# Mamba sample states: streamed past column tiles, updated two sequences at a time

## The reference, cut to what matters

```python
def step(h, inp):
    x_q, dt_q, b_q, c_q = inp
    acum = jnp.cumsum(dt_q * a_gr, axis=1)
    ...
    y = jnp.einsum('bijgr,bjgrp->bigrp', cb[..., None] * lmat, xdt)
    y = y + jnp.einsum('bign,bgrpn->bigrp', c_q, h) * jnp.exp(acum)[..., None]
    to_end = jnp.exp(acum[:, -1:] - acum)
    h = h * jnp.exp(acum[:, -1])[..., None, None] \
        + jnp.einsum('bjgn,bjgrp->bgrpn', b_q, xdt * to_end[..., None])
    return h, y
```

## Time and profile before

| what | value |
|---|---|
| median of the runs | 3171.85 us (3167.19 to 3178.89) |
| the profiled execution's own time (its span, first to last instruction) | 3169.1 us |
| busy share of PE, DVE, ACT, POOL over the span | 85%, 51%, 34%, 6% |
| stretch of the sample part, first read to last add | 1942.9 to 2057.7 us |

### The profile page before, as it was taken

One profiled execution on the slowest core, in us unless ns is written; L12 is line 12 of the kernel. 1 busy time (PEld: TensorE's weight loads), 2 busy tenths in 40 slices (PEclk: granted clock), 3 DMA queues, 4 the chain that ended last, 5 costly groups with the idle time before them and its releaser, 6 DMA issues. The chain is left out here.

```text
span 3169.1 us, 48791 instructions
## 1 busy us (share of the span) xinstructions
PE 2695.0 (85%) x21151; PEld 2385.4 (75%) x21151; DVE 1607.7 (51%) x2358; ACT 1070.8 (34%) x1798; POOL 174.8 (6%) x176
## 2 busy tenths in 40 slices
PE   6939985998847899979989888978997939985999
PEld 5728854998724678869989866678997718864999
DVE  5384336644362577756434843265536374326643
ACT  4333112433311344434334620044434332203442
POOL 0020011000000000000000132200000020011000
PEclk8969867999865899989999965589998978967999
DMA  4210001444200222214434301323442210001442
GB/s 152 90 66 3 6 28 60 153 147 159 98 0 0 67 67 67 67 54 157 149 124 146 138 27 63 131 99 120 147 147 104 83 40 30 6 27 53 147 151 105
DMA packets 44133, 275.70 MB, mean 87 GB/s; under 512 B 5216, under 2 KB 5248, under 8 KB 14096
## 3 DMA queue, kind: packets, MB, share of 16 engines
q1 hardware_dynamic: 43680, 271.95, 24.1%
q0 software_dynamic: 240, 0.64, 0.1%
HBM read 256.32 MB, written 16.24 MB: 86 GB/s over the span
## 5 line engine op out<-in xcount | busy, mean ns | idle before, releaser
L315 PE MATMUL banks<-rounded,rounded 128*128 128x320 f32 x3184 | 1009.8, 317 | 165.3 <-DVE rounded L331 69.1
L316 PE MATMUL banks<-rounded,rounded 128*128 128x320 f32 x3184 | 995.7, 313 | 0.0
L317 PE MATMUL banks<-rounded,rounded 128*128 128x320 f32 x3184 | 995.2, 313 | 0.0
L305 DVE TENSOR_TENSOR rounded<-weight_ring,rounded 128x1024 fp32r<-128x1024 f32 x398 | 487.2, 1228 | 513.4 <-ACT rounded L298 513.1
L315 PEld LDWEIGHTS banks<-rounded,rounded 128*128 128x128 f32 x3184 | 609.4, 191 | 177.3 <-DVE rounded L331 74.3
L316 PEld LDWEIGHTS banks<-rounded,rounded 128*128 128x128 f32 x3184 | 609.7, 191 | 3.6
L317 PEld LDWEIGHTS banks<-rounded,rounded 128*128 128x128 f32 x3184 | 608.8, 191 | 0.0
L298 ACT ACTIVATE rounded<-weight_ring 128x1024 fp32r<-128x1024 f32 x398 | 419.2, 1058 | 414.6 <-PE banks L317 360.1
L942 PE MATMUL banks<-arena 64*64 64x64 f32 x4032 | 146.3, 225 | 22.8 <-PEq L788 20.3
L942 PEld LDWEIGHTS banks<-arena 64*64 64x64 f32 x4032 | 134.4, 140 | 31.0 <-issue 29.2
L470 ACT ACTIVATE arena<-banks 128x320 f32<-128x320 f32 x128 | 56.0, 438 | 247.9 <-PE banks L317 247.9
(11 more groups left out here) (361 smaller groups left out, 3593.1 us busy)
## 6 DMA issues: line engine op xcount, KB each, us to landing
weight_ring<-in_panels SPq DMA_DIRECT2D x206, 1024.0 KB, 4.7
arena<-in_pages SPq DMA_DIRECT2D x64, 320.0 KB, 3.4
arena<-in_ssm SPq DMA_DIRECT2D x8, 1024.0 KB, 4.8
out_ssm_sample<-arena SPq DMA_DIRECT2D x8, 1024.0 KB, 3.8
arena<-in_wkv SPq DMA_DIRECT2D x2, 2048.0 KB, 8.2
out_wkv_sample<-arena SPq DMA_DIRECT2D x2, 2048.0 KB, 6.2
consts<-in_consts SPq DMA_DIRECT2D x1, 1673.5 KB, 9.7
residual<-in_x SPq DMA_DIRECT2D x1, 1280.0 KB, 5.6
```

The source lines that it names most:

```text
L305: self.k.nc.vector.tensor_tensor(self.k.w_lo[:, i % SPLIT], self.raw(i), self.k.w_hi[:, i % SPLIT].bitcast(F32), ALU.subtract)\
L315: mm(out, hi, x_hi, start=start, stop=False)
L316: mm(out, hi, x_lo, start=False, stop=False)
L317: return mm(out, lo, x_hi, start=False, stop=stop)
```

## The change

There are four state buffers: the two old ones, and two more over the first 4096 columns of `XBC`, the convolved inputs, which are last read by the sample chunk's outputs. The sequences go in the order 0, 4, 1, 5, 2, 6, 3, 7, in four pairs.

The read is turned round. The state is the moving operand, 512 columns of a group at a time, and `C` is the weights: for each sequence a 128x32 block per group (`CM`) that holds the eight columns of `C` at the sequence's place among four and zeros elsewhere. The four groups write to four different 32-row strips of one bank, so they sit in four column tiles of the array. The reads of four sequences add up in one bank.

The sums are 32 tokens deep in place of 64: sequence 0 to 3 lie in token rows 0 to 31, sequence 4 to 7 in rows 32 to 63, and a pair takes one of each, in two row tiles, into two banks. Three pairs of banks rotate, and DVE adds 512 columns at a time.

POOL clears and fills `CM` over the prompt state's space after that state's store has landed. Since the reads now come out token by row, ACT copies them to SBUF, PE transposes them, and DVE multiplies them in by four small instructions for each half.

```diff
+    add("seq4", (p[:, None] % 32 // 8 == np.arange(4)[None]))
...
+    HB += [k.at(MB["XBC"] + 2048 * i, MH, 64) for i in range(2)]
+    CM = HT.rearrange("p a b -> p (a b)")[:, 0:1024].rearrange("p (b g t) -> p b g t", b=NB, g=4)
+    YTK = XDT.rearrange("p a b -> p (a b)")[:, 0:1024].rearrange("p (h n) -> p h n", h=2)
+    seqs = [0, 4, 1, 5, 2, 6, 3, 7]
+    sums = [0, 1, 2, 3, 6, 7]
...
-            for b in range(NB):
-                sp.wait_ge(*vec_did.at("HB", b))
-                sp.dma_start(io["ssm_sample"][b], flat(HB[b % 2])).then_inc(state_out[b % 2], 16)
-                if b + 2 < NB:
-                    sp.wait_ge(state_out[b % 2], 16 * (b // 2 + 1))
-                    sp.dma_start(flat(HB[b % 2]), io["ssm"][b + 2]).then_inc(state_in[b % 2], 16)
-            sp.wait_ge(prompt_out, 16)
+            sp.wait_ge(*vec_did.at("y", 2, 7))
+            for s in range(2, 4):
+                sp.dma_start(flat(HB[s]), io["ssm"][seqs[s]]).then_inc(state_in[s], 16)
+            for s in range(NB):
+                sp.wait_ge(*vec_did.at("HB", s, 3))
+                sp.dma_start(io["ssm_sample"][seqs[s]], flat(HB[s % 4])).then_inc(state_out[s % 4], 16)
+                if 1 <= s <= 4:
+                    sp.wait_ge(state_out[s - 1], 16)
+                    sp.dma_start(flat(HB[s - 1]), io["ssm"][seqs[s + 3]]).then_inc(state_in[s - 1], 16)
...
-            for b in range(NB):
-                cols = slice(TP + TS * b, TP + TS * b + TS)
-                pe.wait_ge(state_in[b % 2], 16 * (b // 2 + 1))
-                for f in range(MT):
-                    ins = mm(k.ps[:, 4 + f // 8, (f % 8) * 64 + TS * b:(f % 8) * 64 + TS * b + TS], flat(HB[b % 2])[:, f * P:(f + 1) * P],
-                             XBC[:, 20 + f // 4, cols], start=True, stop=True)
-                ins.then_inc(*pe_did.tick("ys", b))
-                pe.wait_ge(*vec_did.at("bm", b))
-                if b:
-                    pe.wait_ge(*vec_did.at("HB", b - 1))
+            pe.wait_ge(*pool_did.at("cm"))
+
+            def reads(s):
+                b = seqs[s]
+                pe.wait_ge(state_in[s % 4], 16 * (s // 4 + 1))
                 for g in range(4):
-                    ins = mm(k.bank(g), BM[b % 2][0:64, g, :], flat(XDW)[0:64, 512 * g:512 * (g + 1)], start=True, stop=True)
-                ins.then_inc(*pe_did.tick("hb", b))
+                    ins = mm(k.ps[32 * g:32 * g + 32, 4 + b // 4, :], CM[:, b, g, :], flat(HB[s % 4])[:, 512 * g:512 * (g + 1)],
+                             start=b % 4 == 0, stop=b % 4 == 3)
+                ins.then_inc(*pe_did.tick("ys", s))
+
+            def sums_of(pair, g):
+                u = 4 * pair + g
+                if u >= 3:
+                    pe.wait_ge(*vec_did.at("HB", 2 * ((u - 3) // 4) + 1, (u - 3) % 4))
+                for i in range(2):
+                    r = slice(32 * i, 32 * i + 32)
+                    ins = mm(k.bank(sums[u % 3 * 2 + i]), BM[pair % 2][r, g, :], flat(XDW)[r, 512 * g:512 * (g + 1)],
+                             start=True, stop=True)
+                ins.then_inc(*pe_did.tick("hb", pair, g))
...
+            for half in range(2):
+                act.wait_ge(*pe_did.at("ys", 6 + half))
+                s.activation(YTK[:, half, :], k.bank(4 + half), ACT.Copy).then_inc(*act_did.tick("ytk", half))
...
+            pool.wait_ge(prompt_out, 16)
+            g_.memset(flat(HT)[:, 0:1024], 0.0).then_inc(*pool_did.tick("cm0"))
+            pool.wait_ge(*pool_did.at("cm0"))
+            for i in range(4):
+                ins = g_.tensor_copy(CM[:, i::4, :, TS * i:TS * i + TS].rearrange("p b g t -> p g b t"),
+                                     XBC[:, 20:24, TP:T].rearrange("p g (b t) -> p g b t", b=NB)[:, :, i::4, :])
+            ins.then_inc(*pool_did.tick("cm"))
...
+                for g in range(4):
+                    u = 4 * pair + g
+                    vec.wait_ge(*pe_did.at("hb", pair, g))
+                    for i in range(2):
+                        s = 2 * pair + i
+                        if g == 0:
+                            vec.wait_ge(*pool_did.at("hb", s))
+                        part = flat(HB[s % 4])[:, 512 * g:512 * (g + 1)]
+                        v.tensor_tensor(part, part, k.bank(sums[u % 3 * 2 + i]), ALU.add).then_inc(*vec_did.tick("HB", s, g))
```

More of the change, by code:

```diff
@@ L2174, in stage_mamba_scan @@
     act_did, pe_did, vec_did, pool_did = k.tallies("act", "pe", "vec", "pool")
-    state_in = [k.sem("ssm_in_a"), k.sem("ssm_in_b")]
-    state_out = [k.sem("ssm_out_a"), k.sem("ssm_out_b")]
+    state_in = [k.sem(f"ssm_in{i}") for i in range(4)]
+    state_out = [k.sem(f"ssm_out{i}") for i in range(4)]
     prompt_out = k.sem("ssm_prompt_out")
@@ new lines, in _ @@
+            for pair in range(NB // 2):
+                reads(2 * pair)
+                reads(2 * pair + 1)
+                pe.wait_ge(*vec_did.at("bm", pair))
+                for g in range(4):
+                    sums_of(pair, g)
+            for half in range(2):
+                pe.wait_ge(*act_did.at("ytk", half))
+                pe.wait_ge(*vec_did.at("HB", NB - 1, 1))
+                for a in range(4):
+                    ins = nc.tensor.transpose(k.ps[:, 2 + half, a * P:(a + 1) * P], YTK[:, half, a * P:(a + 1) * P], k.const("ident"))
+                ins.then_inc(*pe_did.tick("ysT", half))
@@ L2309, in _ @@
                     g_.tensor_tensor(m, m, bcm(CB[0:n, q // 2, 0:n], 4), ALU.mult).then_inc(*pool_did.tick("m", c, q))
[L2310 to L2312 removed]
+            pool.wait_ge(prompt_out, 16)
[5 more added lines that the diff above has]
+            ins.then_inc(*pool_did.tick("cm"))
+            for s in range(NB):
+                pool.wait_ge(*pe_did.at("ys", s))
+                g_.tensor_tensor(HB[s % 4], HB[s % 4], bc(EE[:, 2 + seqs[s], :], 64), ALU.mult).then_inc(*pool_did.tick("hb", s))
         @block.vector
@@ L2370, in _ @@
             vec.wait_ge(*act_did.at("bt", 2))
[L2371 to L2381, removed]
+            for pair in range(NB // 2):
+                if pair >= 2:
+                    vec.wait_ge(*pe_did.at("hb", pair - 2, 3))
+                v.tensor_scalar(flat(BM[pair % 2])[0:64, :], flat(BT)[0:64, :], k.const("seq4", slice(0, 64))[:, pair:pair + 1],
+                                None, ALU.mult).then_inc(*vec_did.tick("bm", pair))
+                for g in range(4):
+                    u = 4 * pair + g
[6 more added lines that the diff above has]
+                        v.tensor_tensor(part, part, k.bank(sums[u % 3 * 2 + i]), ALU.add).then_inc(*vec_did.tick("HB", s, g))
+            for half in range(2):
+                vec.wait_ge(*pe_did.at("ysT", half))
+                for g in range(4):
+                    ins = v.tensor_tensor(Y[:, 4 * g:4 * g + 4, TP + 32 * half:TP + 32 * half + 32],
+                                          Y[:, 4 * g:4 * g + 4, TP + 32 * half:TP + 32 * half + 32],
+                                          k.ps[:, 2 + half, :].rearrange("p (a g t) -> p a g t", a=4, g=4)[:, :, g, :], ALU.mult)
+                ins.then_inc(*vec_did.tick("ysm", half))
+            vec.wait_ge(*vec_did.at("ysm", 1))
             v.tensor_tensor(Y[:, :, TP:T], Y[:, :, TP:T], YI, ALU.add).then_inc(*vec_did.tick("yfin"))
```

6 lines of the change are left out of this document (3 added, 3 removed).

## The result

The changed kernel takes 3123.15 us (median of 4 runs, 3121.41 to 3125.65), the kernel before on the same chip 3169.52 (median of 4, 3164.15 to 3178.89). The ratio is 0.985, with a 95% interval of 0.983 to 0.987. By that interval the change saves 40 to 55 us; the medians lie 46.4 apart. The forecast was 3121, a saving of 50.6, so the change gained what was forecast to within what these runs can tell.

What follows compares the result with a forecast made beforehand. PE was taken as the bound, eight rounds of 14.05 us. The last add comes 52.3 us earlier, less 1.7 for the last stores, gives 50.6: 3171.85 - 50.6 = 3121 us, range 3104 to 3138.

Steps and rivals of the forecast that it cites:

- likeliest case: Whole kernel: 3121 us, with loads as the bound of the last two pairs; own range 3114 to 3130, chance 0.63.
- Four column tiles together: Reads of a sequence: four column tiles run together, 0.16 + 1.71 = 1.87 us.
- The start: Before the first read: PE waits for `CM`, first read at 1944.8 in place of 1942.98, 1.8 us lost.
- the term of the copies: Building `CM` on POOL: four copies of eight short runs, 0.55 us each, bounds 0.3 and 1.0.
- First two pairs: Pair 0 takes 14.2 us and pair 1 12.0: reads, two rescales 7.24, then seven adds.
- Last two pairs: Pairs 2 and 3: 17.2 us for pair 2, same loop in pair 3; a load stands behind another sequence's store.
- the load's term: Load behind a store, pairs 2 and 3: 7.2 us from the store's issue if they share, otherwise 5.2; 7.2 taken.
- the forecast's chain: Pairs 2 and 3 after the load lands: reads 1.87 + 0.28, one rescale 3.62, seven adds 4.9.
- Loads that never bind: Rival: pairs 2 and 3 take 12.0 us like pair 1, gain 61 (3111); within a rival group of chance 0.14.
- The end: After the last pair: last add at 2005.4, 52.3 us earlier; the last two stores share, 1.7 us lost.
- POOL slowed by DVE's adds: Rival: rescales beside adds take 7.7 us, POOL 15.5 a pair, gain falls to 26 (3146); chance 0.04.
- The clock stays at 0.50: PE through the sample part: clock stays at 0.50; full clock, worth 4 to 5 us more (3106), shares chance 0.14.

Runs made afterwards that it cites:

- one tile alone: The changed kernel with all four groups of reads written to the same 32 columns of TensorE; span 3136.1 us, sample part 84.3 us.
- column tiles alone: The changed kernel with sums, masks and adds in their old form, one sequence at a time; span 3148.1 us, sample part 92.2 us.
- Loads early: The changed kernel with loads five to eight issued ahead of the next pair's stores; 3114.44 us, ratio 0.982 to the kernel before, sample part 55.8 us.
- row tiles alone: The changed kernel with reads in their old form, without `CM` or transposes; span 3150.4 us, sample part 99.1 us.
- same tile in a row: The changed kernel with a pair's reads ordered group by group, both sequences of a group in succession; span 3136.3 us, sample part 82.0 us.

## Why the prediction was right

Its likeliest case came true, step by step. That the total is so close is partly luck: the start and the first pair were 1.7 us too dear, the last two pairs 2.3 too cheap.

- *Four column tiles together*: right. A sequence's reads take 1.94 us by the timeline (forecast 1.87), and one tile alone takes 0.853 us for each of the eight instructions. By the ratio of 3.07 that the Trainium skill (TensorE: Matmul & The Clock Gate, Part 3) gives for four row tiles it would have been an estimated 2.28; the trace is nearer to the ideal.
- *The start*: the term of the copies was too dear, four in 0.96 us and not 2.2. The first read came at 1943.78 and not 1944.8.
- *First two pairs*: 13.5 and 12.0 for 14.2 and 12.0. DVE's adds overlap, seven in 4.28 us and not 4.83.
- *Last two pairs*: 18.3 and 18.4 for 17.2 each. The wait and its cause were right, the size of the load's term was not: three transfers share at that moment and not two, since the second sequence's store goes out 0.85 us behind the first's (1969.62 after 1968.77), on the other side of the load (1969.15). The load landed 8.4 us after the first store's issue and not 7.2. With one store alone, as the forecast had it, the price was right: in the run with column tiles alone, where no second store follows the load, it landed 7.3 us after the store's issue (1963.34 to 1970.65, and the page below, in the columns of the earlier trace rows). In the kernel after, PE's sums at half clock and two adds end last behind the load, and not rescale and seven adds; that is 0.3 us shorter than the forecast's chain.

```profile
arena<-in_ssm SPq DMA_DIRECT2D x8, 1024.0 KB, 6.9
```

- *Loads that never bind*: the forecast's rival put them at a gain of 61. Loads early shows 63.3 by the part's length (119.16 - 55.84).
- *The end*: the last add at 2006.05 for 2005.4; the next stage starts 6.24 us later, 1.82 more than before, for a forecast of 1.7. The part lost 50.65 by its own length and the next stage starts 49.85 earlier, for a forecast of 50.6.
- *POOL slowed by DVE's adds*: did not happen, 3617 ns at most. But the rival had a true core, the other way round and for another instruction: POOL holds DVE's mask. In the kernel after the masks fall between rescales (472 ns), so it costs nothing there.
- *The clock stays at 0.50*: wrong in part. It was 1.00 from 1948.70 to 1952.11 and from 1958.94 to 1965.77, and 0.50 through pairs three and four. In those two stretches the sums are not on the path (they lie beside the rescales), so it moved the time little. Windows inside the two stretches, in the columns of the earlier trace rows:

```profile
1948.70:1952.10 3.40, 2.15 (x10) 0.57 (x8) 0.69 (x1) 0.00 (x0) 3.40 (x2) 1.00 0.26 111
1958.90:1965.80 6.90, 3.13 (x16) 1.06 (x12) 1.42 (x3) 0.00 (x0) 6.13 (x2) 0.99 0.97 372
```

What stayed open: what makes the clock rise here. It rose in the first two pairs of the kernel after and not in the last two, and not at all with row tiles alone, where PE was busy without a break through the first two pairs.

## What to carry to other kernels

When an engine that bound a stage gets nearly three times faster, write down where every transfer is issued, not only how long it takes: here a load that stood behind an unrelated store in one queue was worth 12.7 us, as much as a quarter of the change's gain. Measure parts of a change in a stage's own length, since untouched stages differ by more than many edits are worth. And before an instruction of DVE is moved beside one of POOL, look at where both take their inputs.

## What the runs showed of the hardware

- Four fp32 matmuls in four column tiles start within 0.05 us and take the time of one (0.853 us for an instruction of 512 columns at 1.2 GHz), in both orders of the list that were run.
- A DVE operation of one input, from SBUF to SBUF (64x512 fp32), takes 0.47 us alone and 3.63 beside a POOL operation with two SBUF inputs that started 0.27 us before it; the POOL operation next in line then takes 3.80 in place of 3.62 (column tiles alone). A DVE add with one input in PSUM takes 0.69 either way.
- A load of 1 MB takes 4.8 us alone, 6.9 when issued 0.4 us behind one store (column tiles alone), and 8.1 to 8.2 where a second store follows 0.5 us later (the kernel after).
- With the list interleaved so that neighbours sit in one column tile, reads in four tiles still started together. The fourteenth instruction of the list, which reports the first sequence, was the eighth to start, and its counter rose 2.8 us later, 0.04 us ahead of the other's (same tile in a row).
